# Expert up weights moved by halves of the contraction, w1 and w3 together

## The reference, cut to what matters

```python
def run_block(args):
    toks, gts, e = args
    xb = xt[toks]
    h = jax.nn.silu(xb @ w1[e]) * (xb @ w3[e])
    return (h @ w2[e]) * gts[:, None].astype(xt.dtype)
```

## Time and profile before

| | us |
|---|---|
| median of three runs | 1162.44 (1162.04 to 1164.29) |
| the profiled execution | 1163.39 |
| its span, first to last instruction | 1161.7 |
| TensorE busy in the span | 1003.0 (86%) |
| VectorE busy | 533.1 (46%) |
| ScalarE busy | 399.3 (34%) |
| moved by DMA | 308.93 MB |

### The profile page before, as it was taken

How to read it: one execution, slowest core, us unless ns; L and a number is a source line. 1 busy time by engine, 2 the same in 40 slices (tenths; PEclk the granted TensorE clock), 3 DMA queues, 4 the chain that set the end, 5 groups by cost and what they waited for, 6 DMA issues and landing times. The chain is left out here.

```text
span 1161.7 us, 24427 instructions
## 1 busy us (share of the span) xinstructions
PE 1003.0 (86%) x9062; PEld 698.1 (60%) x9062; DVE 533.1 (46%) x980; ACT 399.3 (34%) x712; POOL 274.4 (24%) x319
## 2 busy tenths in 40 slices
PE   5999999999998999999994799989998786858470
PEld 4888888888886657788884345545454443424230
DVE  5741522111017888655458444352535252444337
ACT  5412233212125667303213344252343343233232
POOL 0101000101000000000000456565656362515120
PEclk9999999999999999999996899999999898979795
DMA  8733331531324003538459899999999999999985
GB/s 302 295 127 118 118 127 45 217 135 47 143 91 155 1 1 146 163 127 323 190 199 413 326 408 415 421 420 418 415 418 419 419 419 417 420 421 420 417 341 221
DMA packets 69427, 308.93 MB, mean 266 GB/s; under 512 B 8376, under 2 KB 8552, under 8 KB 61200
## 3 DMA queue, kind: packets, MB, share of 16 engines
q1 hardware_dynamic: 57008, 273.86, 59.2%
q0 software_dynamic: 12384, 34.63, 7.7%
HBM read 275.68 MB, written 36.44 MB: 269 GB/s over the span
## 5 line engine op out<-in xcount | busy, mean ns | idle before, releaser
L608 PE MATMUL ps<-whi,xTh 128*128 128x512 f32 x480 | 187.8, 391 | 13.8 <-DVE wlo L1267 13.8
L609 PE MATMUL ps<-wlo,xTh 128*128 128x512 f32 x480 | 187.5, 391 | 0.0
L610 PE MATMUL ps<-whi,xTl 128*128 128x512 f32 x480 | 187.4, 390 | 0.0
L902 PE MATMUL ps<-cur13a,xT 128*32 128x256 f32 x1984 | 134.5, 417 | 3.3 <-issue 2.6
L1855 POOL DMA_INDIRECT xg<-xn_scratch,idxb x60 | 96.9, 1615 | 151.9 <-PE ps L891 132.2
L1740 DVE COPY cur13a<-rawe 128x4096 f32 x31 | 71.5, 2306 | 132.9 <-DMA rawe<-in_w 102.0
L926 PE MATMUL ps<-cur,hT 128*32 128x256 f32 x1952 | 118.0, 382 | 8.2 <-issue 7.5
L902 PE MATMUL ps<-cur13b,xT 128*32 128x256 f32 x1984 | 121.2, 385 | 1.4 <-DVEq L1756 0.7
L1230 ACT ACTIVATE cur<-rawe 128x4096 f32 x30 | 108.6, 3621 | 8.5 <-issue 4.9
L1002 ACT ACTIVATE zst<-ps,rstd 128x512 f32<-128x512 f32 x60 | 40.8, 687 | 204.1 <-PE ps L610 197.8
L608 PEld LDWEIGHTS ps<-whi,xTh 128*128 128x128 f32 x480 | 90.6, 189 | 32.6 <-issue 13.7
(11 more groups left out here) (231 smaller groups left out, 1356.8 us busy)
## 6 DMA issues: line engine op xcount, KB each, us to landing
rawe<-in_w SPq DMA_DIRECT2D x96, 2048.0 KB, 31.3
raw<-in_w_in SPq DMA_DIRECT2D x20, 1024.0 KB, 8.0
z_scratch<-zst POOLq DMA_DIRECT2D x60, 256.0 KB, 2.3
gat<-z_scratch SPq DMA_DIRECT2D x12, 512.0 KB, 3.9
xn_scratch<-rrow POOLq DMA_DIRECT2D x6, 1024.0 KB, 5.6
raw<-in_w_out SPq DMA_DIRECT2D x4, 1024.0 KB, 6.5
xcol<-in_x_cols SPq DMA_DIRECT2D x6, 512.0 KB, 9.9
x_scratch<-x SPq DMA_DIRECT2D x6, 512.0 KB, 4.3
```

The source lines that it names most:

```text
L608: pe.matmul(out, ah, bh, start=first, stop=False)
L609: pe.matmul(out, ah, bl, start=False, stop=False)
L610: return pe.matmul(out, al, bh, start=False, stop=last)
L902: mm = pe.matmul(ps[0][u * CAP:(u + 1) * CAP, 0:256], xT[:, c % 2, x:x + CAP], cur13[h][:, :, c * 512 + u * P:c * 512 + (u + 1) * P], star ...
```

## The change

The transfers of w1 and w3 are no longer one each (16 KB a partition) but two each (8 KB a partition), and those of half 0 of w1 and w3 go together, then those of half 1. The slot's layout becomes w1 half 0, w3 half 0, w1 half 1, w3 half 1, w2. Half 0 is sent when half 0 of expert p-3 was copied, half 1 when half 1 was. Each half has a semaphore a slot that counts both its transfers (32), and DVE and ACT wait for the half that they copy.

```diff
--- before.py
+++ after.py
@@ -339,8 +339,8 @@
         s_tbm = sem("s_tbm")
         s_ic = sem("s_ic")
         s_nb = sem("s_nb")
-        s_w1 = [sem(f"s_w1{s}") for s in range(RING)]
-        s_w3 = [sem(f"s_w3{s}") for s in range(RING)]
+        s_wa = [sem(f"s_wa{s}") for s in range(RING)]
+        s_wb = [sem(f"s_wb{s}") for s in range(RING)]
         s_w2 = [sem(f"s_w2{s}") for s in range(RING)]
         s_c13 = sem("s_c13")
         s_cw2 = sem("s_cw2")
@@ -523,27 +523,37 @@
             sp.dma_start(wrt[:, :, :], A["router_w"].rearrange("(p c) n -> p c n", c=KC)).then_inc(s_rp, 16)
             sp.dma_start(brt[:, :], A["router_b"].rearrange("(a n) -> a n", a=1).partition_broadcast(P)[:, 0, :]).then_inc(s_rp, 16)
             sp.dma_start(gcol[:, :], A["ffn_norm_g"][0].rearrange("(p c) -> p c", c=KC)).then_inc(s_rp, 16)
-            def weight(x, slot, k, done):
-                c = slot * EW + k * 2 * PIECE
-                sp.dma_start(rawe[:, c:c + 2 * PIECE].rearrange("p (h n) -> p h n", h=2 if k < 2 else 4),
-                             e_w[k][bass.ds(x, 1)][0]).then_inc(done[slot], 16)
+            def up_half(x, slot, h):
+
+                for k in range(2):
+                    c = slot * EW + (2 * h + k) * PIECE
+                    sp.dma_start(rawe[:, c:c + PIECE],
+                                 e_w[k][bass.ds(x, 1)][0][:, h, :]).then_inc((s_wa, s_wb)[h][slot], 16)
+
+            def down_weight(x, slot):
+
+                c = slot * EW + 4 * PIECE
+                sp.dma_start(rawe[:, c:c + 2 * PIECE].rearrange("p (h n) -> p h n", h=4),
+                             e_w[2][bass.ds(x, 1)][0]).then_inc(s_w2[slot], 16)
 
             def expert(p, x, slot=None):
 
                 held = not isinstance(p, int) or p >= RING
                 slot = p % RING if slot is None else slot
                 if held:
+                    sp.wait_ge(s_c13, 2 if isinstance(p, int) and p == RING else 2 * p - (2 * RING - 1))
+                up_half(x, slot, 0)
+                if held:
                     sp.wait_ge(s_c13, 2 * p - (2 * RING - 2))
-                weight(x, slot, 0, s_w1)
-                weight(x, slot, 1, s_w3)
+                up_half(x, slot, 1)
                 if held:
                     sp.wait_ge(s_cw2, p - (RING - 1))
-                weight(x, slot, 2, s_w2)
+                down_weight(x, slot)
 
             def x2_out(t):
                 sp.dma_start(x2_d[t * P:(t + 1) * P, :], x2[t % 3][:, :]).then_inc(s_x2s[t % 3], 16)
-            for k in (s_w1, s_w3, s_w2):
-                sp.sem_inc(k[2], 16)
+            for k, n in ((s_wa, 32), (s_wb, 32), (s_w2, 16)):
+                sp.sem_inc(k[2], n)
 
             def residual(t):
                 sp.dma_start(xres[t % 3][:, :], x_tiles[t]).then_inc(s_xr[t % 3], 16)
@@ -557,17 +567,17 @@
                 if t < 3:
                     residual(t + 3)
             sp.wait_ge(s_w, 2 * NT - 2)
-            weight(EPG * ORDER[1], 1, 2, s_w2)
-            weight(EPG * ORDER[2], 2, 0, s_w1)
+            down_weight(EPG * ORDER[1], 1)
+            up_half(EPG * ORDER[2], 2, 0)
             sp.wait_ge(s_x2, X2_DONE[NT - 2])
             x2_out(NT - 2)
             sp.wait_ge(s_x2, X2_DONE[NT - 1])
             x2_out(NT - 1)
-            weight(EPG * ORDER[1], 1, 0, s_w1)
-            weight(EPG * ORDER[1], 1, 1, s_w3)
-            weight(EPG * ORDER[2], 2, 1, s_w3)
+            up_half(EPG * ORDER[1], 1, 0)
+            up_half(EPG * ORDER[1], 1, 1)
+            up_half(EPG * ORDER[2], 2, 1)
             sp.wait_ge(s_rr, NT)
-            weight(EPG * ORDER[2], 2, 2, s_w2)
+            down_weight(EPG * ORDER[2], 2)
             expert(3, EPG * ORDER[3])
 
             def number(p):
@@ -1167,10 +1177,9 @@
             route_copy(NT - 1)
 
             def first_up(h):
-                act.activation(cur13[h][:, :, :], rawe[:, 0:4 * PIECE].rearrange("p (k n) -> p k n", k=2)
-                               [:, :, h * PIECE:(h + 1) * PIECE], ACT.Copy).then_inc(s_c13, 1)
-            act.wait_ge(s_w1[0], 16)
-            act.wait_ge(s_w3[0], 16)
+                act.wait_ge((s_wa, s_wb)[h][0], 32)
+                act.activation(cur13[h][:, :, :], rawe[:, 2 * h * PIECE:(2 * h + 2) * PIECE]
+                               .rearrange("p (k n) -> p k n", k=2), ACT.Copy).then_inc(s_c13, 1)
             first_up(1)
             act.wait_ge(s_lg, NT)
             act.wait_ge(s_rr, NT)
@@ -1735,16 +1744,15 @@
 
                 def take(h):
 
-                    pair = rawe[:, bass.ds((e1 % RING) * EW, 4 * PIECE)].rearrange("p (k n) -> p k n", k=2)
+                    landed = (s_wa, s_wb)[h]
+                    dve.wait_ge(landed[0], 32 * (e1 // 3) + 32)
+                    dve.wait_ge(landed[1], 32 * ((e1 + 2) // 3))
+                    dve.wait_ge(landed[2], 32 * ((e1 + 1) // 3) + 32)
                     dve.wait_ge((s_13a, s_13)[h], b + 1)
-                    dve.tensor_copy(cur13[h][:, :, :], pair[:, :, h * PIECE:(h + 1) * PIECE]).then_inc(s_c13, 1)
+                    half = rawe[:, bass.ds((e1 % RING) * EW + 2 * h * PIECE, 2 * PIECE)]
+                    dve.tensor_copy(cur13[h][:, :, :], half.rearrange("p (k n) -> p k n", k=2)).then_inc(s_c13, 1)
 
                 with dve.If(e1 > e):
-
-                    for k in (s_w1, s_w3):
-                        dve.wait_ge(k[0], 16 * (e1 // 3) + 16)
-                        dve.wait_ge(k[1], 16 * ((e1 + 2) // 3))
-                        dve.wait_ge(k[2], 16 * ((e1 + 1) // 3) + 16)
                     take(0)
                 dve.wait_ge(s_c13, 2 * e1 + 1)
                 dve.sem_inc(s_ga, 1)
```

## The result

The changed kernel takes 1164.95 us (median of 21 runs, 1163.87 to 1165.53), the kernel before 1162.29 (21 runs, 1161.26 to 1164.61), ratio 1.0019 with a 95% interval of 1.0013 to 1.0025: slower by 2.2 us by the ratio, 2.7 by the medians. This lies in the range and just inside the 0.2% that I called no change, but on its slow side. My sum had said +0.1.

The account below looks back on a forecast made before the run. The prediction took the DMA stream of weights to bound the experts' stage. Its terms, +3.5 for packets, -0.8 for the dry stretch and -2.6 for the end, summed to +0.1 us, 1162.5 us, range 1158.7 to 1166.5.

Parts of the forecast that it names:

- My sum: Whole kernel: packet cost +3.5, dry stretch -0.8 and end -2.6 give +0.1 us, 1162.5 us.
- What bounds the kernel: Experts' stage: the DMA stream of weights bounds it at 419 to 420 GB/s, not TensorE.
- Part 1: Weight stream from expert 4 on: smaller up-weight pieces cost 7 ns per added packet, +3.5 us.
- lower bound of 0: Weight stream: no loss if an 8 KB packet is as quick per byte as a 16 KB one.
- rival of free packets: Weight stream: a shared rate limit absorbs the fixed cost per packet; -3.4 us, 1159.0; chance 0.22.
- bad pattern: Weight stream: 8 KB pieces run at the pace of 4 KB packets; +7.8 us, 1170.2; chance 0.14.
- transfer of 1 MB: Weight stream, a rival: 1 us unhidden fixed cost each, 56 us for 56 more; chance 0.02.
- Part 2: Dry stretch near 654 to 660 us: expert 4's halves go earlier, the gap mostly moves; -0.8 us.
- Part 3: Last expert and end: take(1) and last scatter 3.4 us earlier, of which 2.6 reach the end; -2.6 us.
- What costs nothing: SP and DVE: additional issues, waits and conditions are hidden by existing waiting; 0 us.
- third rival: End: ya loads do not close up to ye, as the last scatter lands slower; +2.7 us, 1165.1; chance 0.10.

Follow-up runs that it names:

- e1: Kernel before with each w1 and w3 sent as two 8 KB-a-partition transfers, old order and places, all awaited; 1165.91 us, ratio 1.0023 against before.
- e2: Kernel before with one transfer per matrix but the slot laid out by halves, so packets are 8 KB; 1165.61 us, ratio 1.0024 against before.
- e11: Kernel before with w1 and w3 sent as four transfers of 4 KB a partition each, all awaited; 1173.51 us, ratio 1.0099 against before.
- e4: Changed kernel, but DVE waits for both halves before take(0), as the kernel before did; 1165.78 us, ratio 1.0017 against before.
- e7: Kernel before with only experts 4 and 5 sent by halves, expert 5's up halves ahead of expert 4's w2 in SP's list; 1159.63 us, ratio 0.9975.
- e12: Changed kernel with gf's load behind ya and a sixth ye buffer; 1162.31 us, ratio 0.9996 against before.
- e3: Kernel before with three long-met conditions on w3 put before take(1) on DVE; 1163.38 us, ratio 0.9999 against before.
- e5: Kernel before, loading only the first 128 tokens' rows of x2t, residual left out for the others; 1160.02 us, ratio 0.9979 against before.
- e6: Changed kernel, loading only the first 128 tokens' rows of x2t, residual left out for the others; 1161.05 us, ratio 0.9988 against before.
- e8: e7 with gf's load put behind ya; 1158.69 us, ratio 0.9967 against before.

## Why the prediction was right, and where it was not

**What bounds the kernel** held: fewer bytes per busy microsecond made the whole kernel longer by nearly as much as forecast.

**Part 1, +3.5 us: right, slightly high.** e1 and e2 measure 2.7 to 3.2. The term was 7 ns a packet; the two give 5.4 to 6.4 and e11 7.0 to 7.6. The lower bound of 0 and the rival of free packets fall, and so does the bad pattern (12 ns a pair). That a transfer of 1 MB costs nothing of its own is shown by e1 against e2. The Trainium skill (DMA: Bandwidth & Descriptors, Why small descriptors are slow) has about 3 cycles a packet, from which I had estimated 3.5 ns and 1.8 us. The measured price is 1.5 to 2.2 times that, so the trace was the better guide, and the page's sign was right. e1 alone would still allow 3.5 ns; e11, at 6.5 ns or more, does not.

**Part 2, -0.8 us: the mechanism is right, the size is not resolved.** First issue at 653.7 (forecast 655.4; the block ran 1.7 us ahead in this execution), a dip at 666 to 670 (forecast 667 to 670), w2 of expert 4 still behind ACT's copy. e4, which has the earlier release and not the lead, against e1 gives 0.7 us for it, with an uncertainty of 1.5 us. e7 shows the step that held it down: the order of SP's list, and 3.0 us when that is changed too.

**Part 3, -2.6 us: wrong, measured about 0** (e4 against the changed kernel, -0.2 us, with an uncertainty of 1.3 us). Up to the last scatter it went as written: take(1) waits for the DMA, and the scatter comes 3.8 us before that of e4, where 3.4 were forecast. It then failed at the sentence "With the issue at 1130.5 the ya loads stand in the queue right behind ye", by which the fourth ya was to land 5.0 to 5.8 us behind the last ye (1140.2 to 1141.0, and 1135.2). In the changed kernel it landed 6.7 us behind it (1143.6 and 1136.9), and in e4, without the lead, 6.8. Two things are wrong in the step.

First, an earlier issue is not an earlier landing. Of the 3.8 us, 1.7 are lost before the issue, because ya stands in SP's list behind the sixth ye load, and this waits for the first sum. I had read the earlier trace rows for how long the loads take and not for what holds the sixth back. The other 2.1 are nearly all lost between issue and landing, behind the sixth ye load, which was itself issued only 0.4 us before ya. That e12, where the sixth has a buffer, comes down to 5.6 us fits this, but it is a single trace in which gf has moved as well, and single traces differ: e2's, without lead and without the buffer, has 5.9.

Second, the profile from which I counted the gain has something that other executions do not have. In the profile of before the fourth ya landed 7.9 us behind the last ye (1143.1 and 1135.2), but there TensorE's clock had held up the last scatter by 1.7 us. Without this fall and with no lead at all it is 6.8 in e4's profile, 6.7 in e3's and 5.9 in e2's. So 1.1 us or more of the 2.6 were the clock's and not the change's to win.

That the lead gives nothing is shown by e4 (no lead, same time), where it goes by the issues and landings of single profiles. That a freed queue lets it through is suggested by e12, and weakly by e5 and e6; it is not shown.

**What costs nothing** held: e3 finds no cost for the conditions on DVE, e1 against e2 none for SP's additional issues.

**The sum** is then +2.7 to 3.2 for part 1 and -0.5 for parts 2 and 3 together (read as the difference between e1 and the changed kernel, so that the sum closes by construction). The case that came true is the third rival, "The end gives nothing", with 1165.1, to which I had given 0.10. Its reason was not mine (a slower landing of the last scatter: it is 5.5 us to SP's issue in the earlier trace rows and 5.7 in e4 and e12), but the sixth ye load and the queue behind it. The sum of +0.1 missed by 2.1 to 2.6 us, about what part 3 had been given. That the range held the time all the same is luck as far as part 3 goes: the forecast and this rival are only 2.6 us apart.

## What to carry to other kernels

Halving a transfer so that its buffer is given back earlier pays only where the stream runs dry, and then only if the next entries of the same queue can go as well; everywhere else it costs its packets, here 5 to 8 ns for each on its engine. Before counting a lead of the compute at the end, read the list of the queue that it must pass, above all a load in it that waits for a buffer which is no bottleneck yet, and look at TensorE's granted clock there in more than one profile.

## What the runs showed of the hardware

The price of a packet is the same within the noise whether 16 KB are cut into 8 or into 4 KB, and whether the cut makes more transfers or only more packets, while the DMA share stays at 1.02 to 1.03. TensorE's granted clock fell to its lower level for about 3.4 us in the last expert's up product in the profile of before, and so it did in e5's, the second window here, but not in the changed kernel's or e4's:

```profile
1114.00:1116.20 2.20, 0.63 (x9) 1.00 1.00 408
1116.20:1119.60 3.40, 3.40 (x40) 0.50 0.69 278
```

From the last take(1) to the last scatter it is 12.2 to 12.3 us in the profiles of before, e1, e5 and e8, which have the fall, and 10.1 to 10.6 us in the other ten, which do not. One such fall adds 1.7 us to the path at the end, more than half of what this whole study had to tell apart, and it is in some executions and not in others: a lead that is read from two single traces has this uncertainty. How often it comes was not looked at, nor whether it is why the 21 runs of before lie 3.4 us apart and those of the changed kernel 1.7.
